# GpSimd multiplies both key pages of a step with the queries in the cached attention, VectorE only sums the products

## The chip, the cores and the metric

The kernel runs on one core of a Trainium2 chip. The core has five engines, each with its own in-order instruction stream: TensorE (matrix products, PE in the profile), VectorE (DVE), ScalarE (ACT), GpSimd (POOL) and SyncE (SP, which here issues most DMAs). They wait for each other through semaphores. The metric is the device time of one execution in microseconds (us), the median of several runs.

## What is computed

One inference step of a decoder layer with two parallel branches, in float32, for a prompt of 1024 tokens and for 8 samples that each continue a cached context of 4096 tokens. The change touches the attention of the 8 samples over their paged cache alone; of the reference that is

```python
def _diff_attend(q, k, v, q_pos, k_pos, lam):
    s = jnp.einsum('nqhmd,nkhmd->nhmqk', q, k).astype(jnp.float32) * (A_DH ** -0.5)
    mask = k_pos[None, :] <= q_pos[:, None]
    p = jax.nn.softmax(jnp.where(mask, s, -jnp.inf), axis=-1)
    p = p[:, :, 0] - lam * p[:, :, 1]
    return jnp.einsum('nhqk,nkhe->nqhe', p.astype(v.dtype), v)
...
        past_k = cache_k[l][page_table].reshape(n_dec, past_len, A_HEADS, A_HD)
        past_v = cache_v[l][page_table].reshape(n_dec, past_len, A_HEADS, A_HD)
```

For each sample there is one query of 4 heads with two sub-queries of 64 each (8 dot products of length 64 with each cached key), 32 pages of 128 keys, and the new key of the step itself. The rest of the layer is a projection of all tokens to 36 blocks of 128 features ("dense"), a causal attention of the prompt with itself, a short convolution with a chunked delta-rule recurrence ("prep" and "solve", 8 tiles of 128 tokens), gates, an output projection, and a recurrent update for the samples.

## The kernel before

Work is staged in three parts that matter here. A first part normalises the tokens and projects queries, keys and values of the prompt (to about 230 us). Then two stages run several streams of work at once. In the first (about 230 to 720 us) they are the dense projection of 20 feature blocks, the attention of the prompt (four heads), and the cached attention of samples 0 to 3. In the second (about 720 to 1310 us) they are the 16 remaining feature blocks, the recurrence with its prep and solve, and the cached attention of samples 4 to 7. The order in which the streams' pieces come is written out once (`phase_a`, `phase_b`, which weave the streams' steps evenly), and every engine goes through this same order with its own share of each piece. Since an engine is in-order, a wait in one stream holds up all others on that engine. A last part (from about 1310 us) projects up, gates and writes the results.

The cached attention (`cached` in each engine's block) takes 16 steps a sample, `gp = j * 16 + i` for step i of sample j, 128 in all. A step covers two key pages, an even and an odd one:

- SyncE loads the two pages into a ring of three pairs (`kring`, semaphores `kin0` to `kin2`). It loads pair gp+3 once both products of gp have been made (`even_mul` and `odd_mul`, L394 and L395). Behind that in its queue come the value pages (ring of six, `load_v`, freed by TensorE's `v_used`), the query broadcasts and the weights of the dense projection.
- GpSimd multiplies the even page (128 keys on partitions, 512 features) with the sample's query, which is broadcast to all partitions (`qB`), into the ring `prod` of four slots, two for each page of two steps (L581). It waits for the even reduction two steps back, which frees its slot.
- VectorE multiplies the odd page in the same way (L1091), then sums the even product in groups of 64 to 8 scores a key (L1093) and the odd one (L1095).
- After 16 steps VectorE adds the score of the step's own key (L1101 to L1103, which write slot 1 of `prod`) and takes the maximum (L1106, `sc_ready`). TensorE and ScalarE do the softmax and the weighted sum of the value pages (L1454) during the next sample's steps.

What stands in the same queues near the change: GpSimd copies the tail of each convolved block (L567, L568), once ScalarE has filled the convolution's buffer (L781); takes powers for the norms (L591, L601, L624); and makes the products of a recurrence tile (L606 to L608, L611 and L612, L615 and L616). VectorE does the convolution's three taps (L1071: multiply a shifted buffer by a weight and add it to the sum, both in SBUF) after ScalarE's L750, the last product of the silu (L1077), the prompt attention's maxima (L1152 to L1154) and combination (L1159 to L1161), and the solve's L1244 to L1268. ScalarE's exponentials are L817, its evacuations L825 to L830. TensorE's dense product is L1425, the prompt attention's L1486, L1499 and L1520, prep's L1542, solve's L1539.

Of the kernel before, what the change touches and what calls it, by code (L numbers as in the profile page):

```python
# [7 lines left out]
ALU = mybir.AluOpType  # L8
# [68 lines left out]
def _program(nc, a, ctx):  # L77
# [65 lines left out]
    s = Semaphores()  # L143
# [31 lines left out]
    kring = sa[:, 0:3072].rearrange("p (u n) -> p u n", u=RK)  # L175
    vring = sa[:, 3072:6168].rearrange("p (u h n) -> p u h n", u=RV, h=AH)
    prod = sa[:, 6168:8216].rearrange("p (u n) -> p u n", u=4)
    qB = sa[:, 8216:9240].rearrange("p (u n) -> p u n", u=2)
# [86 lines left out]
    def v3(ap, n):  # L265
        return ap.rearrange("p (g d) -> p g d", g=n)
# [277 lines left out]
    def _(po):  # L544
# [27 lines left out]
        def cached():  # L572
            for j in range(NS + 1):
                for i in range(SA_STEPS):
                    if j < NS:
                        gp = j * 16 + i
                        po.wait_ge(s["qb_in"], 16 * (j + 1))
                        po.wait_ge(s[f"kin{gp % 3}"], 32 * (gp // 3 + 1))
                        if gp >= 2:
                            po.wait_ge(s["even_red"], gp - 1)  # L580
                        nc.gpsimd.tensor_tensor(prod[:, 2 * (gp % 2), :], kring[:, 2 * (gp % 3), :], qB[:, j % 2, :], ALU.mult).then_inc(s["even_mul"], 1)  # L581
                    yield
            for _ in range(4):
                yield
# [34 lines left out]
        def solve():  # L619
            for t in range(NT):  # L620
                for i in range(SOLVE):
# [3 lines left out]
                    yield  # L625

        gens = dict(dense=dense(), sa=cached(), att=att(), prep=prep(), solve=solve())
        run(ORDER_A, gens)
        run(ORDER_B, gens)
# [327 lines left out]
    def _(dve):  # L957
        nv = [0]

        def link(ins):  # L960
            nv[0] += 1
            ins.then_inc(s["v"], 1)
            dve.wait_ge(s["v"], nv[0])
# [121 lines left out]
        def cached():  # L1085
            def scores(j, i):
                gp, par = j * 16 + i, j % 2
                o = 2 * (gp % 2)
                dve.wait_ge(s["qb_in"], 16 * (j + 1))
                dve.wait_ge(s[f"kin{gp % 3}"], 32 * (gp // 3 + 1))  # L1090
                nc.vector.tensor_tensor(prod[:, o + 1, :], kring[:, 2 * (gp % 3) + 1, :], qB[:, par, :], ALU.mult).then_inc(s["odd_mul"], 1)  # L1091
                dve.wait_ge(s["even_mul"], gp + 1)
                nc.vector.tensor_reduce(sc[:, par, 2 * i, :], v3(prod[:, o, :], 8), AX_X, ALU.add).then_inc(s["even_red"], 1)  # L1093
                dve.wait_ge(s["odd_mul"], gp + 1)
                nc.vector.tensor_reduce(sc[:, par, 2 * i + 1, :], v3(prod[:, o + 1, :], 8), AX_X, ALU.add).then_inc(s["odd_red"], 1)  # L1095

            def maximum(j):
                par = j % 2
                dve.wait_ge(s["odd_red"], 16 * (j + 1))
                dve.wait_ge(s["self_k"], 16 * (j + 1))  # L1100
                nc.vector.tensor_tensor(prod[0:1, 1, :], kself, qB[0:1, par, :], ALU.mult).then_inc(s["self_used"], 1)  # L1101
                dve.wait_ge(s["self_used"], j + 1)
                link(nc.vector.tensor_reduce(sc[0:1, par, NPAGE, :], v3(prod[0:1, 1, :], 8), AX_X, ALU.add))  # L1103
                if j:
                    dve.wait_ge(s["mT_ready"], j)
                nc.vector.tensor_reduce(mx1[:], sc[:, par].rearrange("p g e -> p e g"), AX_X, ALU.max).then_inc(s["sc_ready"], 1)  # L1106

            def softmax(j, i):
                if i == 1:
                    dve.wait_ge(s["mT_ready"], j)  # L1110
                    link(nc.vector.tensor_reduce(mx8[:], ps[0:8, 6, 0:P], AX_X, ALU.max))
                    nc.vector.tensor_scalar(diag8[:], ident[0:8, 0:8], mx8[:], None, ALU.mult).then_inc(s["diag_ready"], 1)
                if i == 3:
                    dve.wait_ge(s["mB_ready"], j)
                    if j >= 2:
                        dve.wait_ge(s["pr_ready"], j - 1)
                    nc.vector.tensor_tensor(scx, sc[:, 1 - j % 2], ps[:, 6, P:P + 8].unsqueeze(1).to_broadcast([P, PAGES, 8]), ALU.subtract).then_inc(s["scx_ready"], 1)

            def combine(m, i):
                if i == 0:  # L1120
                    dve.wait_ge(s["pv_done"], m + 1)
                    if m:
                        dve.wait_ge(s["comb_ready"], m)
                    link(nc.vector.reciprocal(rl[:], ps[:, 7, HD:HD + 1]))
                    nc.vector.tensor_scalar(on[:], ps[:, 7, 0:HD], rl[:], None, ALU.mult).then_inc(s["on_ready"], 1)
                if i == 3:
                    dve.wait_ge(s["comb_ready"], m + 1)
                    nc.vector.tensor_copy(oTs[:, :, m:m + 1], ps[:, 6, 136:136 + AH].unsqueeze(2)).then_inc(s["oTs_ready"], 1)

            for j in range(NS + 1):  # L1130
                for i in range(SA_STEPS):
                    if j >= 2:
                        combine(j - 2, i)
                    if j >= 1:
                        softmax(j, i)
                    if j < NS:
                        scores(j, i)
                        if i == SA_STEPS - 1:
                            maximum(j)
                    yield  # L1140
            for i in range(4):
                combine(NS - 1, i)
                yield
# [644 lines left out]
```

## Time and profile before

| | us |
|---|---|
| runs | 1601.95, 1602.59, 1603.6 |
| median | 1602.59 |
| the profiled execution | 1601.74 |
| its span in the profile | 1600.0 |

The profile is one execution, seen by the hardware profiler. Its span goes from the first instruction to the last; 1.74 us of the execution's own time lie around it. Busy times of engines overlap. A wait is idle time of an engine, put down to what ended it. A duration on VectorE or GpSimd includes the time that the instruction stood still after its start.

### The profile page before, as it was taken

The numbers are of one execution on the slowest core, as the hardware profiler recorded it, in microseconds if no ns is written. First come the engines' busy times: TensorE is split into PE (matmuls) and PEld (weight loads), VectorE is DVE, ScalarE is ACT, GpSimd is POOL, SyncE is SP. The second block draws the span as 40 slices with busy tenths as digits, with TensorE's granted clock in tenths as the row PEclk, the third lists the DMA queues.
The fourth block names the chain that finished last, engine by engine and source line by source line (L and its number), as shares of the span: only waits on it lengthen the run. The fifth ranks groups of instructions, "written<-read, shape, count | busy, mean of one in ns | idle before, by whom it ended". The sixth has DMA issues, their size and how long they took to land.

```text
span 1600.0 us, 23081 instructions
## 1 busy us (share of the span) xinstructions
PE 1422.1 (89%) x8089; PEld 937.1 (59%) x8089; DVE 796.6 (50%) x1411; ACT 297.5 (19%) x850; POOL 357.0 (22%) x257
## 2 busy tenths in 40 slices
PE   3999999988988988986788988989999958959998
PEld 3444866655555555554466766767677745636443
DVE  4546126676776686554565565765533212263001
ACT  2122123223323323222111111121121100000000
POOL 0123101121222131113424324252321100270000
PEclk9999999999999999997999999999999988889999
DMA  7022214444663763665774766767534048214121
GB/s 246 5 83 93 102 52 137 144 128 133 218 204 111 221 215 122 214 212 182 236 241 135 241 201 180 232 186 218 166 113 120 14 156 272 88 44 131 63 79 54
DMA packets 235442, 239.74 MB, mean 150 GB/s; under 512 B 19217, under 2 KB 182902, under 8 KB 234806
## 3 DMA queue, kind: packets, MB, share of 16 engines
q1 hardware_dynamic: 228558, 214.93, 44.0%
q10 hardware_dynamic: 6768, 23.34, 3.7%
q8 instruction: 64, 1.05, 0.3%
q14 instruction: 52, 0.43, 0.1%
HBM read 206.06 MB, written 32.25 MB: 149 GB/s over the span
## 4 chain that ended last, share of the span: by engine, by line
PE 66%; DVE 11%; issue 9%; POOL 5%; DMA 3%; ACT 3%; SPq 2%; DVEq 0%; ACTq 0%; POOLq 0%
PE ps L1425 20%; PE ps L1539 7%; PE ps L1398 7%; PE ps L1708 7%; PE ps L1659 7%; PE ps L1408 4%; PE ps L1486 3%; DVE tr L1071 3%; PE ps L1454 3%; POOL sa L581 2%; DMA sa<-in_cache_v 2%; PE ps L1520 2%; PE ps L1542 1%; DVE sm L1153 1%; PE ps L1364 1%
## 5 line engine op out<-in xcount | busy, mean ns | idle before, releaser
L1425 PE MATMUL ps<-hT,r 128*128 128x344 f32 x1728 | 582.1, 473 | 0.8 <-ACT gb L717 0.8
L1425 PEld LDWEIGHTS ps<-hT,r 128*128 128x128 f32 x1728 | 316.1, 197 | 154.5 <-issue 44.4
L581 POOL TENSOR_TENSOR sa<-sa 128x512 f32<-128x512 f32 x128 | 174.5, 1374 | 336.2 <-DVE sa L1093 305.1
L1398 PE MATMUL ps<-r,hT 128*128 128x512 f32 x256 | 112.2, 593 | 0.0
L1708 PE MATMUL ps<-r,hT 128*128 128x512 f32 x256 | 110.3, 592 | 0.0
L1093 DVE TENSOR_REDUCE sa<-sa 128x8 f32<-128x512 f32 x128 | 86.9, 679 | 43.3 <-POOL sa L581 43.3
L1091 DVE TENSOR_TENSOR sa<-sa 128x512 f32<-128x512 f32 x128 | 102.6, 801 | 2.8 <-DMA sa<-in_cache_k 2.3
L1659 PE MATMUL ps<-tr,r 128*128 128x344 f32 x192 | 66.2, 492 | 42.0 <-DVE hT L1286 22.1
L1454 PE MATMUL ps<-sa 128*2 128x129 f32 x2048 | 77.9, 274 | 24.7 <-DMA sa<-in_cache_v 24.6
L817 ACT ACTIVATE r<-ps,sm 128x128 f32<-128x128 f32 (+7 forms) x64 | 47.1, 739 | 217.7 <-DVE sm L1154 217.7
L1539 PEld LDWEIGHTS ps<-r 128*128 128x128 f32 x576 | 74.0, 193 | 23.1 <-DVE r L1253 5.4
L1095 DVE TENSOR_REDUCE sa<-sa 128x8 f32<-128x512 f32 x128 | 86.4, 675 | 0.0
L1539 PE MATMUL ps<-r 128*128 128x128 f32 x576 | 79.0, 281 | 6.6 <-DVE r L1253 3.9
L1708 PEld LDWEIGHTS ps<-r,hT 128*128 128x128 f32 x256 | 48.6, 190 | 60.9 <-issue 60.7
L1486 PE MATMUL ps<-r 64*128 64x512 f32 (+3 forms) x192 | 67.7, 535 | 16.2 <-ACT r L817 16.2
L1398 PEld LDWEIGHTS ps<-r,hT 128*128 128x128 f32 x256 | 47.6, 190 | 55.6 <-issue 55.6
L1454 PEld LDWEIGHTS ps<-sa 128*2 128x2 f32 x2048 | 41.6, 83 | 64.9 <-DMA sa<-in_cache_v 35.0
L1659 PEld LDWEIGHTS ps<-tr,r 128*128 128x128 f32 x192 | 39.1, 207 | 63.1 <-issue 47.0
L1244 DVE TENSOR_TENSOR tr<-ps,tr 128x512 f32<-128x512 f32 x48 | 33.1, 690 | 85.0 <-PE ps L1539 84.9
L1071 DVE SCALAR_TENSOR_TENSOR tr<-tr,convw 128x1024 f32<-128x1024 f32 x36 | 57.9, 1610 | 22.1 <-ACT tr L750 21.2
L1351 DVE SCALAR_TENSOR_TENSOR tr<-ps,tabs 128x1024 f32<-128x1024 f32 x8 | 9.8, 1225 | 103.6 <-PE ps L1708 103.6
L1659 PE MATMUL ps<-r 128*128 128x344 f32 x192 | 60.2, 457 | 0.0
(265 smaller groups left out, 1768.5 us busy)
## 6 DMA issues: line engine op xcount, KB each, us to landing
sa<-in_cache_k SPq DMA_DIRECT2D x256, 256.0 KB, 3.0
sa<-in_cache_v SPq DMA_DIRECT2D x256, 256.0 KB, 3.5
r<-in_w_f SPq DMA_DIRECT2D x36, 512.0 KB, 4.8
g_dram<-tr ACTq DMA_DIRECT2D x16, 516.0 KB, 4.0
cv_dram<-tr ACTq DMA_DIRECT2D x12, 512.0 KB, 3.0
sa<-g_dram SPq DMA_DIRECT2D x16, 344.0 KB, 3.3
tr<-cv_dram SPq DMA_DIRECT2D x20, 256.0 KB, 4.5
r<-in_x_prompt SPq DMA_DIRECT2D x8, 512.0 KB, 5.0
```

The costliest lines, as they stand in the source:

```text
L581: nc.gpsimd.tensor_tensor(prod[:, 2 * (gp % 2), :], kring[:, 2 * (gp % 3), :], qB[:, j % 2, :], ALU.mult).then_inc(s["even_mul"], 1)
L1071: ins = nc.vector.scalar_tensor_tensor(y, ub[:, k:k + SEQ], convw[:, n, k:k + 1], y, ALU.mult, ALU.add)
L1091: nc.vector.tensor_tensor(prod[:, o + 1, :], kring[:, 2 * (gp % 3) + 1, :], qB[:, par, :], ALU.mult).then_inc(s["odd_mul"], 1)
L1093: nc.vector.tensor_reduce(sc[:, par, 2 * i, :], v3(prod[:, o, :], 8), AX_X, ALU.add).then_inc(s["even_red"], 1)
L1095: nc.vector.tensor_reduce(sc[:, par, 2 * i + 1, :], v3(prod[:, o + 1, :], 8), AX_X, ALU.add).then_inc(s["odd_red"], 1)
L1398: ins = nc.tensor.matmul(ps[:, n % 4, :], hT[:, k, t * P:(t + 1) * P], wt[c][:, k, :], start=(k == 0), stop=(k == KD - 1))
L1425: ins = nc.tensor.matmul(ps[:, 4 + i % 2, 0:G3], wf[f % 4][:, k * P:(k + 1) * P], hT[:, k, cg * G3:(cg + 1) * G3], start=(k == 0), stop=(k ...
L1454: ins = nc.tensor.matmul(ps[32 * h:32 * h + 2, 7, 0:HD + 1], pr[:, p, 2 * h:2 * h + 2], vring[:, v % RV, h, :], start=(p == 0), stop=False ...
L1486: ins = nc.tensor.matmul(ps[:, (m if qb < 4 else 0) + c0 // 512, 0:c1 - c0], QT[r, h, qb * P:(qb + 1) * P], KT[r, h, c0:c1], start=True, s ...
L1539: return heads(lambda o, c: nc.tensor.matmul(o, lhsT[:, c], rhs[:, c], start=True, stop=True), bank)
L1659: ins = nc.tensor.matmul(ps[:, 2 * (n % 2) + m, 0:G3], wup[f][:, (m * AH + k) * P:(m * AH + k + 1) * P], src[:, k, cols], start=(k == 0), ...
L1708: ins = nc.tensor.matmul(ps[:, b0 + hf, :], yT[:, k, t * P:(t + 1) * P], wout[:, k, hf * W:(hf + 1) * W], start=(k == 0), stop=(k == KD - 1))
```

## The change

GpSimd makes the odd product too, right after the even one, and VectorE only sums. GpSimd therefore gets a wait for the odd reduction two steps back, and at the first step of each sample but the first a wait for the sample's maximum before, since the score of the step's own key is worked out in slot 1 of `prod`. VectorE's waits for the query and the key pair go with its multiply. SyncE's code is the same, but `odd_mul` now comes from GpSimd.

```diff
@@ -579,6 +579,11 @@
                         if gp >= 2:
                             po.wait_ge(s["even_red"], gp - 1)
                         nc.gpsimd.tensor_tensor(prod[:, 2 * (gp % 2), :], kring[:, 2 * (gp % 3), :], qB[:, j % 2, :], ALU.mult).then_inc(s["even_mul"], 1)
+                        if gp >= 2:
+                            po.wait_ge(s["odd_red"], gp - 1)
+                        if j and i == 0:
+                            po.wait_ge(s["sc_ready"], j)
+                        nc.gpsimd.tensor_tensor(prod[:, 2 * (gp % 2) + 1, :], kring[:, 2 * (gp % 3) + 1, :], qB[:, j % 2, :], ALU.mult).then_inc(s["odd_mul"], 1)
                     yield
             for _ in range(4):
                 yield
@@ -1086,9 +1091,6 @@
             def scores(j, i):
                 gp, par = j * 16 + i, j % 2
                 o = 2 * (gp % 2)
-                dve.wait_ge(s["qb_in"], 16 * (j + 1))
-                dve.wait_ge(s[f"kin{gp % 3}"], 32 * (gp // 3 + 1))
-                nc.vector.tensor_tensor(prod[:, o + 1, :], kring[:, 2 * (gp % 3) + 1, :], qB[:, par, :], ALU.mult).then_inc(s["odd_mul"], 1)
                 dve.wait_ge(s["even_mul"], gp + 1)
                 nc.vector.tensor_reduce(sc[:, par, 2 * i, :], v3(prod[:, o, :], 8), AX_X, ALU.add).then_inc(s["even_red"], 1)
                 dve.wait_ge(s["odd_mul"], gp + 1)
```

## Rows read from the trace of the kernel before

**Rows 1.** Busy time of each engine in the two stages (start:end, length, engines).
```profile
core 0: us, PE busy (x) PEld busy (x) DVE busy (x) ACT busy (x) POOL busy (x), PEclk, DMA share, GB/s
230.00:720.00 490.00, 449.85 (x2409) 275.72 (x2409) 332.57 (x540) 143.31 (x368) 102.20 (x91) 0.96 0.55 170
720.00:1170.00 450.00, 394.21 (x3039) 294.18 (x3040) 261.61 (x487) 79.81 (x297) 154.54 (x117) 0.94 0.66 199
```
**Rows 2.** The page's costliest groups: busy, mean ns, idle before and its enders.
```profile
L581 POOL TENSOR_TENSOR sa<-sa 128x512 f32<-128x512 f32 x128 | 174.5, 1374 | 336.2 <-DVE sa L1093 305.1
...
L1091 DVE TENSOR_TENSOR sa<-sa 128x512 f32<-128x512 f32 x128 | 102.6, 801 | 2.8 <-DMA sa<-in_cache_k 2.3
```
**Rows 3.** Single lines of code: duration ns minimum/median/maximum.
```profile
L581 POOL TENSOR_TENSOR sa<-sa x128: 1257/1271/2260, 176.0 to 1134.4; 128x512 f32<-128x512 f32 x128
...
L1091 DVE TENSOR_TENSOR sa<-sa x128: 668/686/1774, 228.9 to 1139.3; 128x512 f32<-128x512 f32 x128
...
L1093 DVE TENSOR_REDUCE sa<-sa x128: 666/679/687, 229.5 to 1139.9; 128x8 f32<-128x512 f32 x128
...
L1071 DVE SCALAR_TENSOR_TENSOR tr<-tr,convw x36: 1283/1475/2184, 331.4 to 617.9; 128x1024 f32<-128x1024 f32 x36
```
**Rows 4.** Waits in the first stage (230 to 720): total us, times, longest.
```profile
PE ps L1486 <- ACT r L817: 16.2, 4, 4.5
PE ps L1520 <- ACT junk L830: 15.8, 5, 5.0
...
PE ps L1499 <- DVE r L1161: 1.2, 3, 0.6
```
**Rows 5.** One stall of TensorE in the timeline, from 458 to 467.
```profile
458.09 0.19 POOL L567 COPY utail<-tr 128x3 f32<-128x3 f32 x1 [7.88 <-ACT tr L781]
...
458.37 3.49 POOL L581 TENSOR_TENSOR sa<-sa 128x512 f32<-128x512 f32 x2
...
466.22 0.80 PE L1486 MATMUL ps<-r 64*128 64x256 f32 x2 [4.48 <-ACT r L817]
```
**Rows 6.** The chain of work that ended last, in the same stall (start, us, what).
```profile
459.24 1.49 DVE tr L1071
...
460.76 2.19 DVE tr L1071
...
462.97 1.28 DVE tr L1071
```
**Rows 7.** Waits in the second stage (720 to 1170): total us, times, longest.
```profile
DVE sa L1093 <- POOL sa L581: 43.3, 20, 3.2
...
PE ps L1454 <- DMA sa<-in_cache_v: 22.3, 24, 3.5
...
PE ps L1539 <- DVE r L1247: 9.0, 11, 3.0
...
PE ps L1542 <- DVE tr L1264: 4.4, 1, 4.4
...
PE ps L1539 <- DVE r L1253: 3.9, 2, 2.5
...
PE ps L1539 <- POOL r L616: 1.7, 1, 1.7
```
**Rows 8.** Timeline of another convolution block, 434 to 442: multiplies and taps.
```profile
435.72 4.46 POOL L581 TENSOR_TENSOR sa<-sa 128x512 f32<-128x512 f32 x2
...
435.53 5.73 DVE L1071 SCALAR_TENSOR_TENSOR tr<-tr,convw 128x1024 f32<-128x1024 f32 x3
```
**Rows 9.** Timeline around a late step of the second stage, 851 to 854.
```profile
851.46 0.69 DVE L1093 TENSOR_REDUCE sa<-sa 128x8 f32<-128x512 f32 x1 [2.50 <-POOL sa L581]
...
852.66 0.68 DVE L1264 TENSOR_TENSOR tr<-ps,sm 128x512 f32<-128x512 f32 x1
...
853.39 0.48 PE L1542 MATMUL ps<-ident,tr 128*128 128x128 f32 x1 [4.42 <-DVE tr L1264]
```
**Rows 10.** SyncE's own waits over the whole run: total us, times, longest.
```profile
SPq L395 <- DVE sa L1091: 239.0, 63, 9.2
```
**Rows 11.** Busy time and granted clock right after one stall.
```profile
466.00:472.50 6.50, 6.11 (x13) 3.27 (x14) 6.33 (x14) 2.15 (x8) 1.27 (x1) 0.50 0.48 152
```

## The prediction

> **What bounds the kernel now.** I read the stages first. In the two stages that hold all 128 score steps TensorE is busy 449.85 of 490 us and 394.21 of 450 us [rows 1]: it sets the pace and waits only now and then. VectorE is busy 332.57 and 261.61 us in them, GpSimd 102.20 and 154.54 us, so neither is full. What the change can be worth is therefore read from TensorE's idle time and from who ends it, not from the busy sums.
>
> Next, the costs of one step. GpSimd's multiply stands at 174.5 us for 128, VectorE's at 102.6 us for 128 [rows 2]. Undisturbed, GpSimd's takes 1271 ns and VectorE's 686 ns, but both reach far higher: 2260 and 1774. The reductions never do (666 to 687), and VectorE's convolution taps at L1071, which have two SBUF operands like the multiplies, spread from 1283 to 2184 [rows 3]. So a GpSimd multiply and a VectorE instruction with two SBUF operands delay each other; one with a single SBUF operand is left alone.
>
> Then TensorE's waits. In the first stage nearly all are two kinds: four of 16.2 us behind ScalarE's exponentials and five of 15.8 us behind its L830 [rows 4]. In the trace these are six stalls of 4.5 to 5.0 us (and three short ones), all of one make, of which [rows 5] show one: GpSimd sits in its in-order queue at the copy L567 until ScalarE has filled the convolution buffer; that same event starts VectorE's three taps; GpSimd then runs its two overdue multiplies into the taps. The chain of waits shows what that does: 1.49, 2.19 and 1.28 us [rows 6]. The middle tap has lost 0.9 us. Behind the taps VectorE does the row maxima that the exponentials wait for, and only after those the next score step. In the second stage TensorE waits 22.3 us in 24 pieces for value pages, and 19.0 us behind VectorE's and GpSimd's share of the chunked recurrence (L1247, L1253, L1264, L616). There VectorE also waits 43.3 us in 20 pieces for GpSimd's even multiply [rows 7]: late steps, in which GpSimd's queue had the tile preparation in front.
>
> **What is removed.** 128 multiplies leave VectorE, 102.6 us. Worth is only what of this TensorE waits for. In the six stalls nothing: no L1091 lies between the taps and the maxima, and the taps start when ScalarE's L750 has finished, so earlier savings on VectorE are lost in that wait. Elsewhere in the first stage TensorE waits for VectorE directly for 1.2 us in three pieces (L1161) [rows 4]; I take 0.6. In the second stage eleven waits for L1247 make 9.0 us [rows 7]; two long ones stand behind a late step, where L1091 ran during the wait for GpSimd anyway; the nine others may gain at most 0.69 each, and not more than their own length, so I take 0.2 each, 1.8. Relief: 2.4 us. Its ends are 0 and, if every wait for VectorE or GpSimd in the second stage shrank by 0.69 us (15 pieces) and the 1.2 went, 11.6.
>
> **What is added in the first stage.** GpSimd does two multiplies a step, so four are overdue at each L567, not two. They alternate with the taps, as two back-to-back multiplies already do in another block, where both later taps are hit and the three take 5.73 us [rows 8] instead of the 1.49 + 2.19 + 1.28 = 4.96 of the stall [rows 6]. In the six stalls this hits the last tap too: 2.19 − 1.28 = 0.9 us each, 6 × 0.9 = 5.4 us, straight into TensorE's wait. The six other blocks have no stall, and what their taps lose (0 to 1.8 us) goes into TensorE's work. Lower end 0 (the extra multiplies come after the taps); upper end 3 × 1.27 less the 4.96 − 3 × 1.283 = 1.11 already lost, 2.7 a stall, 16 us.
>
> The Trainium skill ("SBUF — State Buffer", Who interferes with whom) states a rule against this change: a GpSimd instruction and a VectorE one with two SBUF inputs lock the shared port for a whole instruction, and the later one stands still until then. Here the second tap shows 0.9 us lost, less than the multiply's 1.27 us; by the whole instruction the six stalls would give 6 × 1.27 = 7.6 us, an estimate from that page.
>
> **What is added in the second stage.** VectorE now needs even and odd product. Where GpSimd is ahead both are there. In a late step the odd one comes 1.27 us after the even one, of which the even reduction hides 0.6: the step ends 0.65 us later than now. Five of TensorE's stalls stand right behind such a step (one for L1264, two for L1253, two for L1247): 3.3 us. [Rows 9] show one: VectorE waits 2.50 us for GpSimd, reduces twice, does L1264, and TensorE has waited 4.42. In one tile the added multiply stands in front of L615 and L616, for which TensorE waits 1.7 us [rows 7]: 1.3 more. Together 4.6. Ends: 0, and 20 × 1.27 = 25.4 if every late step passes on all of it.
>
> In bursts (three steps in a row behind L606 to L608) the sum is near zero: two multiplies are 2.54 us a step, but VectorE today needs up to 1.77 + 2 × 0.6 = 2.97 there, since it is its own multiply that is blocked (1774 ns [rows 3]; two reductions start to end of turn take 1.2 [rows 9]).
>
> **Waits and queues.** Before each odd multiply GpSimd now waits for the odd reduction two steps back, and once a sample for the maximum (sc_ready). Behind these on GpSimd stand the powers L591 and L601, the tile's products and the copies L567; VectorE, TensorE and ScalarE wait for them. The odd reduction ends 0.6 us after the even one that GpSimd waits for today, the maximum a step ahead of its use, and GpSimd idles over 300 us waiting for VectorE [rows 2], so I cost both at nothing; without that cover it is 7 samples × 1.27 = 8.9 us. SyncE fetches the pages of step gp+3 once both products of gp exist, the value pages behind. Today it waits there 239.0 us for VectorE's multiply [rows 10]; with GpSimd up to two steps ahead it mostly goes on sooner. In late steps it goes on later; I take two such steps at 0.65, 1.3 us, between a loss of 25.4 and a gain of the whole 22.3.
>
> **Sum.** 5.4 + 4.6 + 1.3 − 2.4 = +8.9 us. The profiled execution took 1601.74 us (span 1600.0 and 1.74 around it), so 1610.6; it lies 0.85 below the median of 1602.59, which makes 1611.5. I say 1611.
>
> One cost has no row: TensorE's clock. After such a stall its granted clock is 0.50 for some 6.5 us [rows 11], the lower of its two levels. Whether 0.9 us more idle time lengthens that stretch can't be read off; half as long again, 3.25 us at half speed, costs 1.63 each, 9.8 us for six. I take nothing and keep 9.8 for the range.
>
> **Rivals.**
>
> *GpSimd becomes the bound in the second stage.* Every late step passes on the whole 1.27 us and the clock falls for longer: 5.4 + 25.4 + 9.8 = 40.6 us, 1643; with half of the last two 23 us, 1626. For it: 20 late steps in 64 at half the load. Against: it idles in 295 of those 450 us [rows 1], and 14 of the 20 have no TensorE stall behind them.
>
> *Faster: the key ring lets SyncE go.* If the 239.0 us at L395 are what makes the value pages late, these come sooner and the 22.3 us of waits go: 1602.59 + 5.4 + 4.6 − 2.4 − 22.3 = 1588. It decides from the point where more than half of them go. Against: in front of most of these waits SyncE last waited for TensorE to free a slot, or for nothing.
>
> *No change.* The lost 0.9 us are made good by relief: the stalls fall into a stretch at half clock where TensorE runs slowly anyway, and the late steps gain what L1091 cost. Then 1602.6, give or take 3.2 (0.2%, what a measurement here can tell from none).
>
> **Chances.** Forecast (1606 to 1619) 0.55; GpSimd the bound 0.14; no change 0.17; faster 0.14. So slower 0.69, same 0.17, faster 0.14. The range, 1600 to 1626, leaves about one in ten on each side: it takes in the case of no change with relief near its upper end, and reaches up to GpSimd as the bound at half its price.
>
> **What the profile after would show.** GpSimd near 350 us in 256 multiplies; L1071 at 5.8 to 5.9 us a block instead of 4.96 in the six stalls, and these 5.4 to 5.9 long; VectorE waiting for GpSimd at both reductions, more than 43.3 us together; SyncE's 239.0 us gone from VectorE. The prediction is wrong if the taps don't lengthen, if the stalls stay at 4.5 to 5.0, or if the waits for value pages shrink by over 10 us.

## The result and the profile after

The changed kernel took 1615.65 us in the median of its runs (1612.6 to 1617.12), the kernel before 1602.27 beside it: a ratio of 1.0081 with a 95% interval of 1.0062 to 1.0101, slower by some 13 us. One run of the kernel before, made beside later experiments at a granted clock of 0.736, took 1907.55 us; it is left out of all medians and ratios. The profiled execution took 1614.23 us, its span is 1612.4 us and its mean granted clock 0.946 (before: 1600.0 and 0.953).

First the page's costliest groups that touch the change, after (busy us, mean ns, idle before):

```profile
L581 POOL TENSOR_TENSOR sa<-sa 128x512 f32<-128x512 f32 x128 | 172.1, 1344 | 236.9 <-DVE sa L1095 211.2
L586 POOL TENSOR_TENSOR sa<-sa 128x512 f32<-128x512 f32 x128 | 186.8, 1459 | 2.0 <-DVE mx L1108 2.0
L1095 DVE TENSOR_REDUCE sa<-sa 128x8 f32<-128x512 f32 x128 | 86.9, 679 | 62.4 <-POOL sa L581 62.2
...
L1097 DVE TENSOR_REDUCE sa<-sa 128x8 f32<-128x512 f32 x128 | 86.8, 678 | 16.9 <-POOL sa L586 16.4
...
L1076 DVE SCALAR_TENSOR_TENSOR tr<-tr,convw 128x1024 f32<-128x1024 f32 x36 | 69.7, 1935 | 26.2 <-ACT tr L755 25.3
```

GpSimd now spends 172.1 + 186.8 us in 256 multiplies, against 174.5 in 128 [rows 2]. VectorE has lost its 102.6 us of multiplies and waits 62.2 + 16.4 us for GpSimd's two products. And a line that the diff doesn't touch has changed: the convolution's taps, L1071 before and L1076 now, took 57.9 us on the page of before and take 69.7. Single durations of the taps after (minimum/median/maximum ns):

```profile
L1076 DVE SCALAR_TENSOR_TENSOR tr<-tr,convw x36: 1284/2170/2197, 331.7 to 623.2; 128x1024 f32<-128x1024 f32 x36
```

The median has gone from 1475 [rows 3] to 2170 ns while minimum and maximum stand: the slow tap, rarer than the fast one before, is now the usual one. The two stages after, in the form of [rows 1] (their bounds are moved by the delay so far):

```profile
core 0: us, PE busy (x) PEld busy (x) DVE busy (x) ACT busy (x) POOL busy (x), PEclk, DMA share, GB/s
230.00:726.00 496.00, 448.39 (x2409) 275.04 (x2409) 310.33 (x475) 142.40 (x366) 201.10 (x154) 0.96 0.53 166
726.00:1182.00 456.00, 394.16 (x3041) 295.53 (x3042) 215.56 (x423) 80.01 (x297) 223.78 (x180) 0.94 0.64 196
```

TensorE does the same work. GpSimd is busy 201.10 of 496 us and 223.78 of 456, so it is nowhere the bound. What has grown is TensorE's idle time. Its waits in the first stage, in the form of [rows 4]:

```profile
PE ps L1488 <- ACT r L822: 20.1, 6, 5.5
PE ps L1522 <- ACT junk L835: 18.8, 5, 5.9
PE ps L1501 <- ACT tr L830: 2.6, 2, 1.3
PE ps L1501 <- DVE r L1163: 2.2, 4, 1.2
PE ps L1522 <- ACT tr L830: 1.7, 3, 0.8
```

The first two lines were 16.2 and 15.8 us; their longest pieces have gone from 4.5 and 5.0 us to 5.5 and 5.9. The stall of [rows 5], in the timeline after:

```profile
461.35 0.19 POOL L567 COPY utail<-tr 128x3 f32<-128x3 f32 x1 [5.40 <-ACT tr L786]
...
461.62 1.27 POOL L581 TENSOR_TENSOR sa<-sa 128x512 f32<-128x512 f32 x1
...
462.50 5.88 DVE L1076 SCALAR_TENSOR_TENSOR tr<-tr,convw 128x1024 f32<-128x1024 f32 x3 [1.54 <-ACT tr L755]
...
462.85 2.25 POOL L586 TENSOR_TENSOR sa<-sa 128x512 f32<-128x512 f32 x1
...
465.06 2.24 POOL L581 TENSOR_TENSOR sa<-sa 128x512 f32<-128x512 f32 x1
...
467.26 2.24 POOL L586 TENSOR_TENSOR sa<-sa 128x512 f32<-128x512 f32 x1
...
470.48 0.80 PE L1488 MATMUL ps<-r 64*128 64x256 f32 x2 [5.49 <-ACT r L822]
```

Behind the copy stand four multiplies, and three of them run against the three taps, which take 5.88 us. The chain of waits gives the taps one by one:

```profile
462.50 1.48 DVE tr L1076
...
464.01 2.18 DVE tr L1076
...
466.22 2.17 DVE tr L1076
```

The first two are those of [rows 6] within 0.01; the third has gone from 1.28 to 2.17. In the second stage (720 to 1182), TensorE's waits and VectorE's for GpSimd, in the form of [rows 7]:

```profile
DVE sa L1095 <- POOL sa L581: 62.2, 21, 4.7
...
PE ps L1456 <- DMA sa<-in_cache_v: 20.7, 23, 3.6
...
DVE sa L1097 <- POOL sa L586: 14.7, 30, 0.6
...
PE ps L1541 <- DVE r L1249: 9.0, 11, 2.9
...
PE ps L1541 <- DVE r L1255: 6.9, 3, 2.7
...
PE ps L1544 <- DVE tr L1266: 6.2, 2, 4.7
...
PE ps L1541 <- POOL r L621: 2.5, 1, 2.5
...
PE ps L1541 <- DVE r L1270: 2.2, 1, 2.2
```

The last five lines, TensorE's waits for VectorE and GpSimd, make 26.8 us. Before it was 19.3: the 19.0 of the lines in [rows 7] and 0.3 behind L1250. So +7.5. The late step of [rows 9], after:

```profile
857.12 1.26 POOL L586 TENSOR_TENSOR sa<-sa 128x512 f32<-128x512 f32 x1
857.20 0.69 DVE L1095 TENSOR_REDUCE sa<-sa 128x8 f32<-128x512 f32 x1 [3.01 <-POOL sa L581]
...
858.42 0.69 DVE L1097 TENSOR_REDUCE sa<-sa 128x8 f32<-128x512 f32 x1 [0.54 <-POOL sa L586]
859.02 0.68 DVE L1266 TENSOR_TENSOR tr<-ps,sm 128x512 f32<-128x512 f32 x1
...
859.76 1.11 PE L1544 MATMUL ps<-ident,tr 128*128 128x128 f32 x4 [4.71 <-DVE tr L1266]
```

From the first reduction to the solve's subtraction it takes 859.02 − 857.20 = 1.82 us; in [rows 9] it was 1.20. Between the two reductions VectorE waits 0.54 us for the odd product. Last, SyncE's wait before the key pages, in the form of [rows 10]:

```profile
SPq L395 <- POOL sa L586: 141.8, 42, 12.3
```

For comparing runs I cut the span at three events of the timeline: the first dense product, the first TensorE instruction after the one long wait at the change of stage (for a DMA; 17.9 us before, 18.0 after), and the start of the last dense product. The first stage then takes 509.7 us before and 516.7 after, the second 569.9 and 575.4; the head loses 0.8 and what follows gains 0.7. So +7.0 and +5.5. TensorE's waits, all its idle spells above 0.15 us but that long one, are 38.3 us in the first stage and 44.3 in the second before, and 46.8 and 50.2 after: +8.5 and +5.9. They don't give the stage's length alone, since TensorE also works at a granted clock of 0.50 for part of each stage.

### The profile page after: what moved, and what is told of

It is laid out like the page before. It is cut to its first block, busy times and chain, and to the rows that moved or that the text cites. A ratio compares the mean times of both kernels' runs of the same rounds, so it can differ in the third digit from the quotient of the medians.

```text
span 1612.4 us, 22966 instructions
## 1 busy us (share of the span) xinstructions
PE 1419.8 (88%) x8089; PEld 936.4 (58%) x8089; DVE 728.4 (45%) x1283; ACT 297.3 (18%) x850; POOL 528.5 (33%) x385
## 4 chain that ended last, share of the span: by engine, by line
PE 65%; DVE 11%; issue 8%; POOL 6%; DMA 4%; ACT 3%; SPq 3%; DVEq 0%; ACTq 0%; POOLq 0%
PE ps L1427 20%; PE ps L1400 7%; PE ps L1710 7%; PE ps L1541 7%; PE ps L1661 7%; DVE tr L1076 4%; PE ps L1410 3%; PE ps L1488 3%; PE ps L1456 2%; PE ps L1522 2%; POOL sa L586 2%; DMA sa<-in_cache_v 1%; POOL sa L581 1%; PE ps L1544 1%; DVE sm L1155 1%
## 5 line engine op out<-in xcount | busy, mean ns | idle before, releaser
L581 POOL TENSOR_TENSOR sa<-sa 128x512 f32<-128x512 f32 x128 | 172.1, 1344 | 236.9 <-DVE sa L1095 211.2
L586 POOL TENSOR_TENSOR sa<-sa 128x512 f32<-128x512 f32 x128 | 186.8, 1459 | 2.0 <-DVE mx L1108 2.0
L1095 DVE TENSOR_REDUCE sa<-sa 128x8 f32<-128x512 f32 x128 | 86.9, 679 | 62.4 <-POOL sa L581 62.2
L1661 PE MATMUL ps<-tr,r 128*128 128x344 f32 x192 | 67.0, 497 | 42.0 <-DVE hT L1288 22.1
L1456 PE MATMUL ps<-sa 128*2 128x129 f32 x2048 | 77.6, 276 | 20.9 <-DMA sa<-in_cache_v 20.7
L1097 DVE TENSOR_REDUCE sa<-sa 128x8 f32<-128x512 f32 x128 | 86.8, 678 | 16.9 <-POOL sa L586 16.4
L1076 DVE SCALAR_TENSOR_TENSOR tr<-tr,convw 128x1024 f32<-128x1024 f32 x36 | 69.7, 1935 | 26.2 <-ACT tr L755 25.3
L1456 PEld LDWEIGHTS ps<-sa 128*2 128x2 f32 x2048 | 42.2, 84 | 60.0 <-DMA sa<-in_cache_v 29.3
L559 POOL TENSOR_TENSOR sm<-sm,half 128x8 f32<-128x8 f32 (+1 forms) x17 | 29.1, 1709 | 108.9 <-DVE sm L1028 108.9
L1488 PEld LDWEIGHTS ps<-r 64*128 64x128 f32 x192 | 26.8, 193 | 58.6 <-issue 35.1
```

The lines of the kernel that those rows point to most:

```text
L586: nc.gpsimd.tensor_tensor(prod[:, 2 * (gp % 2) + 1, :], kring[:, 2 * (gp % 3) + 1, :], qB[:, j % 2, :], ALU.mult).then_inc(s["odd_mul"], 1)
L1076: ins = nc.vector.scalar_tensor_tensor(y, ub[:, k:k + SEQ], convw[:, n, k:k + 1], y, ALU.mult, ALU.add)
L1456: ins = nc.tensor.matmul(ps[32 * h:32 * h + 2, 7, 0:HD + 1], pr[:, p, 2 * h:2 * h + 2], vring[:, v % RV, h, :], start=(p == 0), stop=False ...
L1488: ins = nc.tensor.matmul(ps[:, (m if qb < 4 else 0) + c0 // 512, 0:c1 - c0], QT[r, h, qb * P:(qb + 1) * P], KT[r, h, c0:c1], start=True, s ...
L1661: ins = nc.tensor.matmul(ps[:, 2 * (n % 2) + m, 0:G3], wup[f][:, (m * AH + k) * P:(m * AH + k + 1) * P], src[:, k, cols], start=(k == 0), ...
```

## The experiments

All lengths of stages below are of the profiled execution, cut in the same way. One execution gives them to some 3 us: kernels that do the same in the first stage as after take 516.7 to 519.7 us there, and those that do the same in the second 573.4 to 575.8.

| kernel | first stage | second stage | all taps | ratio to before (95% interval) |
|---|---|---|---|---|
| before | 509.7 | 569.9 | 57.9 | |
| after | 516.7 | 575.4 | 69.7 | 1.0081 (1.0062 to 1.0101) |
| first stage only | 517.5 | 569.8 | 69.7 | 1.0044 (1.0028 to 1.0059) |
| second stage only | 510.1 | 575.8 | 57.9 | 1.003 (1.0018 to 1.0042) |
| no odd product | 504.7 | 560.5 | 57.3 | 0.9866 (0.9846 to 0.9886) |
| even product twice | 539.2 | 593.1 | 69.7 | 1.0302 (1.0274 to 1.033) |
| copies on ScalarE, after | 502.6 | 573.4 | 50.2 | 0.9966 (0.9951 to 0.9981) |
| copies on ScalarE, before | 503.9 | 570.4 | 46.8 | 0.9943 (0.9923 to 0.9962) |
| VectorE makes both products | 503.7 | 565.6 | 46.2 | 0.9895 (0.987 to 0.9919) |
| own slot for the self score | 519.7 | 573.4 | 69.7 | 1.0072 (1.0046 to 1.0098) |
| odd product unread | 517.7 | 570.6 | 69.7 | 1.0039 (1.0024 to 1.0054) |
| no odd product, gate kept | 507.9 | 564.1 | 57.2 | 0.9947 (0.9927 to 0.9966) |
| both on VectorE, copies on ScalarE | 503.0 | 567.6 | 46.2 | 0.99 (0.9876 to 0.9924) |

**The two halves apart.** The change for samples 0 to 3 alone (the second kernel has the two conditions the other way round):

```diff
+                        if gp < 64:
+                            if gp >= 2:
+                                po.wait_ge(s["odd_red"], gp - 1)
...
+                            nc.gpsimd.tensor_tensor(prod[:, 2 * (gp % 2) + 1, :], kring[...], qB[...], ALU.mult).then_inc(s["odd_mul"], 1)
...
+                if gp >= 64:
+                    dve.wait_ge(s["qb_in"], 16 * (j + 1))
+                    dve.wait_ge(s[f"kin{gp % 3}"], 32 * (gp // 3 + 1))
+                    nc.vector.tensor_tensor(prod[:, o + 1, :], kring[...], qB[:, par, :], ALU.mult).then_inc(s["odd_mul"], 1)
```

> GpSimd makes the odd product in the first stage alone (samples 0 to 3), VectorE in the second. My theory: the extra multiplies lengthen the taps of the six stalls, 5.7 us as the changed kernel's own trace shows, and little else; 1602.3 + 7 = 1609 us, the six stalls 5.4 to 5.9 us long, the second stage as before. Rival, the loss comes from the second stage alone (late steps) and the first stage's is made good by VectorE's relief: 1602.

> GpSimd makes the odd product in the second stage alone (samples 4 to 7). My theory: late steps end 0.65 us later, 5 stalls behind them, 1.3 for L616 and some for late pages: 1602.3 + 5.5 = 1608 us, the six stalls of the first stage at 4.5 to 5.0 us as before. If both stages' costs simply add, this and the run of the first stage alone together lose the 13 us of the whole change. Rival: GpSimd bound, the second stage carries nearly all of the 13 us: 1615.

They took 1611.82 and 1609.09 us, the kernel before 1603.81 beside them: +0.44% and +0.30%, together +0.74%, within the interval of the whole. Each half lengthens its own stage alone (517.5 and 575.8 us) and leaves the other as it was, so the losses are two and independent.

**VectorE's relief without GpSimd's load.** No engine makes the odd product:

```diff
-                        sp.wait_ge(s["odd_mul"], gp + 1)
...
+        nc.vector.memset(prod, 0.0)
...
-                dve.wait_ge(s["qb_in"], 16 * (j + 1))
-                dve.wait_ge(s[f"kin{gp % 3}"], 32 * (gp // 3 + 1))
-                nc.vector.tensor_tensor(prod[:, o + 1, :], kring[...], qB[:, par, :], ALU.mult).then_inc(s["odd_mul"], 1)
...
-                dve.wait_ge(s["odd_mul"], gp + 1)
```

> The kernel before without any odd product: VectorE's multiply L1091 is left out, the odd reduction sums a zeroed buffer (the scores of the odd keys are left out), SyncE waits for the even product alone. It shows VectorE's relief by itself. My theory: 2.4 us, 1600 us, at most 11.6, 1591. Rival, the key ring lets SyncE go: waits for value pages fall by over 10 us and the time is below 1588.

1584.74 us against 1603.81, 19 us less by the medians and 1.3% or 21 us by the ratio, far more than the 2.4 us of relief in the prediction's sum. But the edit also opens SyncE's gate, so it does two things at once. A later kernel keeps the gate where VectorE's multiply had put it, by making SyncE wait for the even reduction:

```diff
                         sp.wait_ge(s["even_mul"], gp + 1)
-                        sp.wait_ge(s["odd_mul"], gp + 1)
+                        sp.wait_ge(s["even_red"], gp + 1)
                         load_k(gp + 3)
```

> The run without an odd product gained some 20 us, more than the 2.4 that I gave VectorE's relief and more than my upper end of 11.6. This kernel leaves the odd product out in the same way, but SyncE's fetch of the next key pair waits for VectorE's even reduction of the step, as late as VectorE's odd multiply let it go before. If the gain came from the gate of the key ring, it is gone: 1600 and waits for value pages at 22 us again. If it came from VectorE's relief and the multiplies that no longer collide (and the granted clock that follows), it stays: 1585.

1595.39 us against 1603.6, a ratio of 0.9947: the relief alone is worth 8.5 us, and the open gate the rest, some 11 to 13 us. (Relief is here all that goes with VectorE's multiplies, their collisions with GpSimd's too.) The wait at the gate, first in the run that keeps it and then in the one that opens it (both from 230 to 1170):

```profile
SPq L395 <- DVE sa L1090: 244.9, 66, 11.9
```

```profile
SPq L337 <- POOL sa L579: 106.7, 36, 12.2
```

In the same window before, the wait is 233.9 us (239.0 over the whole run [rows 10]), so the first kernel does what it was meant to; in the second the wait is less than half as long. The six stalls are 4.47 to 4.99 us in both, as before. With the gate kept, TensorE's waits in the two stages fall by 4.2 us, from 82.6 to 78.4; the rest of the gain shows as granted clock. Summed over the stretches at 0.50, the first stage has 53.0 us of it before, 47.0 with the gate kept and 57.4 with it open, the second 39.1, 31.5 and 27.9. Whether the relief brings this is not shown: these are single executions, and the mean granted clock of all runs is 0.950 both before and with the gate kept.

**GpSimd's load without the relief.** GpSimd makes the even product twice, VectorE keeps its multiply:

```diff
+                        link(nc.gpsimd.tensor_tensor(prod[:, 2 * (gp % 2), :], kring[...], qB[...], ALU.mult))
                         nc.gpsimd.tensor_tensor(prod[:, 2 * (gp % 2), :], kring[...], qB[...], ALU.mult).then_inc(s["even_mul"], 1)
```

> The kernel before, but GpSimd makes each even product twice into the same slot (nothing left out, VectorE keeps its odd multiply). It adds GpSimd's 1.27 us a step without the relief and without the new waits on reductions and maximum. My theory: the taps meet the same four multiplies, so the six stalls grow by 5.7 us, and each late step by the whole 1.27: 1602.3 + 7 + 8 = 1617. Rival, it is the added waits (odd reduction, maximum) that cost: then about 1604 and stalls as before.

1652.91 us, 3% above before, and well off what was expected. The six stalls are just those of after (5.49 to 5.88 us, all taps 69.7), so it is GpSimd's occupancy that lengthens the taps, with no part in it of the new waits for the odd reduction and the maximum, which this kernel doesn't have. But its stages are 22.5 and 17.7 us longer than those of after, from which it differs by VectorE's multiplies and by one thing more: the even reduction waits here for both of GpSimd's multiplies, in after for the first alone. In its page VectorE's multiplies have grown too, from a mean of 801 ns [rows 2]:

```profile
L1092 DVE TENSOR_TENSOR sa<-sa 128x512 f32<-128x512 f32 x128 | 111.7, 873 | 0.3
```

So with GpSimd doubly loaded the kernel without VectorE's multiply is 40 us shorter (37 by the medians), not 8.5: relief and load don't simply add. TensorE's waits are 18.5 us shorter there (97.0 against 115.5 in the two stages), and its time at 0.50 is 37.5 us less (99.0 against 136.5), by estimate some 19 us at half speed. What of it comes from collisions and what from the later even product these runs don't tell.

**The burst in front of the taps.** GpSimd's two copies, behind which its multiplies pile up, go to ScalarE, which has just filled that buffer; once in the kernel after and once in the one before:

```diff
-                    po.wait_ge(s["f_evac_act"], 3 * (n + 1))
-                    nc.gpsimd.tensor_copy(utail[...], ub[:, SEQ:SEQ + 3].unsqueeze(2))
-                    nc.gpsimd.tensor_copy(sfeat[:, f - 1, :], ub[:, 3 + SEQ:3 + TOK]).then_inc(s["tail"], 1)
...
+            nc.scalar.activation(utail[...], ub[:, SEQ:SEQ + 3].unsqueeze(2), ACT.Copy)
+            nc.scalar.activation(sfeat[:, f, :], ub[:, 3 + SEQ:3 + TOK], ACT.Copy).then_inc(s["tail"], 1)
```

> The changed kernel, with the two small copies L567 and L568 moved from GpSimd to ScalarE, behind its L755 product. GpSimd no longer sits in front of the convolution, so its multiplies are not overdue when the taps start. My theory: the three taps fall from 5.9 us a block towards 3.85, the six stalls from 5.5 to 5.9 us to about 4, so 6 x 1.7 = 10 us off 1615: 1605, less if the copies on ScalarE delay what follows. Rival, the multiplies come when VectorE's reductions free their slots, copies or not: taps and stalls as they are, 1615.

> The kernel before with the same move of the two copies. My theory: taps from 5.0 to 3.85 us in the six stalls, 6 x 1.1 = 6.7 us off: 1596, and the change then costs less than it did. Rival: no effect, 1602, or slower by what the copies cost ScalarE.

1599.69 and 1596.07 us (before: 1604.96). TensorE's two main waits of the first stage, with the change and without it:

```profile
PE ps L1485 <- ACT r L819: 15.0, 4, 5.3
PE ps L1519 <- ACT junk L832: 12.5, 5, 3.9
```

```profile
PE ps L1483 <- ACT r L814: 14.0, 4, 4.4
PE ps L1517 <- ACT junk L827: 12.5, 5, 3.9
```

Both are now shorter than the 16.2 and 15.8 of before [rows 4], and nearly alike; of the six stalls one is longer with the change (5.3 us against 4.4), the others are 3.4 to 3.9 in both. The longer one is the only stall in front of which two multiplies still run into the taps (2300 and 2169 ns). TensorE's waits in the first stage are 31.5 us with the change and 30.2 without, where the copies on GpSimd made it 46.8 and 38.3. So of 8.5 us that the change added to them 1.3 are left: nearly all of its loss there goes through the copies' place in GpSimd's queue. What stays besides that stall is VectorE's wait L1160 (2.4 us, without the change L1158 with 1.0). The lengths of the stage, 502.6 and 503.9, may flatter the change: its execution has only 48.2 us at a clock of 0.50, the other 57.6. By the medians the change now costs 3.6 us, about what its second half alone cost; the second stage takes 573.4 us against 570.4.

**All products on VectorE.** The opposite of the change, so that GpSimd has no share in the scores:

```diff
-                        nc.gpsimd.tensor_tensor(prod[:, 2 * (gp % 2), :], kring[...], qB[...], ALU.mult).then_inc(s["even_mul"], 1)
...
+                nc.vector.tensor_tensor(prod[:, o, :], kring[...], qB[:, par, :], ALU.mult).then_inc(s["even_mul"], 1)
                 nc.vector.tensor_tensor(prod[:, o + 1, :], kring[...], qB[:, par, :], ALU.mult).then_inc(s["odd_mul"], 1)
```

> The other way round: VectorE makes both products, GpSimd none. VectorE gets 88 us more, GpSimd loses 174. If TensorE waits for collisions and late steps and not for VectorE's busy time, as I hold, both go: six stalls at about 3.9 us (6.7 us off), the late steps' 0.65 to 3 us off, but each step on VectorE is 0.69 us longer where it is on the path: 1590 to 1598. Rival, VectorE's load counts: it is busy 33 of 40 us in parts of the first stage, so 128 x 0.69 us more on it cost tens of us: 1620 or more.

1588.59 us, a ratio of 0.9895, just below the 1590 to 1598 that were expected: it beats both kernels, though VectorE has 128 multiplies more. The taps and TensorE's waits in the first stage:

```profile
L1066 DVE SCALAR_TENSOR_TENSOR tr<-tr,convw x36: 1276/1285/1286, 333.9 to 614.7; 128x1024 f32<-128x1024 f32 x36
```

```profile
PE ps L1482 <- ACT r L812: 12.9, 4, 3.4
PE ps L1516 <- ACT junk L825: 12.5, 5, 3.9
PE ps L1495 <- DVE r L1157: 4.6, 4, 1.7
```

All 36 taps take 1276 to 1286 ns: none is slow when GpSimd multiplies nothing. The price of the fuller VectorE stands in the third line (1.2 before), and it is smaller than the gain in the six stalls (3.39 to 3.90 us each). But that is not the whole of the 16 us. Over the two stages TensorE's waits fall only from 82.6 to 78.9 us (those for value pages grow from 22.3 to 26.5 in the second), while its time at 0.50 falls from 92.1 to 71.6, by estimate some 10 us at half speed. This isn't the one execution alone: over all its runs the mean granted clock is 0.956, against 0.951 before. So more of this gain is granted clock than shorter waits, and what raised the clock isn't shown: moving the copies alone in the kernel before shortened the stalls as well and left the mean at 0.949. To this version the move of the copies was added:

> VectorE makes both products and the two copies L567 and L568 are on ScalarE, the two edits that gained alone. My theory: both remove the same burst of GpSimd multiplies into the taps, so the second adds nothing: 1588, stalls at 3.4 to 3.9 us as with either. Rival, their gains of some 17 and 9 us add: 1580.

1587.92 us against 1603.6, a ratio of 0.99, no more than without it, with the same stalls (3.39 to 3.90 us) and the same mean clock of 0.956: the burst can be removed only once.

**The wait for the maximum.** The step's own score is worked out in place instead of in slot 1 of `prod`, so that GpSimd needn't wait for the maximum:

```diff
-                        if j and i == 0:
-                            po.wait_ge(s["sc_ready"], j)
...
-                nc.vector.tensor_tensor(prod[0:1, 1, :], kself, qB[0:1, par, :], ALU.mult).then_inc(s["self_used"], 1)
+                link(nc.vector.tensor_tensor(kself, kself, qB[0:1, par, :], ALU.mult))
+                nc.vector.tensor_reduce(sc[0:1, par, NPAGE, :], v3(kself, 8), AX_X, ALU.add).then_inc(s["self_used"], 1)
...
-                link(nc.vector.tensor_reduce(sc[0:1, par, NPAGE, :], v3(prod[0:1, 1, :], 8), AX_X, ALU.add))
```

> The changed kernel, with the score of the step's own key worked out in place in its own row, so GpSimd needs no wait for the maximum (sc_ready). My theory: the wait had cover, no difference beyond noise, 1615. Rival, the wait holds GpSimd's queue up once a sample: up to 7 x 1.27 = 8.9 us off, 1606.

1615.68 us, a ratio of 1.0072: the time of after. The wait costs nothing that can be measured, as the 2.0 us behind L1108 in the page of after already say.

**The wait for the odd product.** GpSimd makes it as in after, but VectorE sums the query in its place, a tile of the same size, and so never waits for it:

```diff
-                dve.wait_ge(s["odd_mul"], gp + 1)
-                nc.vector.tensor_reduce(sc[:, par, 2 * i + 1, :], v3(prod[:, o + 1, :], 8), AX_X, ALU.add).then_inc(s["odd_red"], 1)
+                nc.vector.tensor_reduce(sc[:, par, 2 * i + 1, :], v3(qB[:, par, :], 8), AX_X, ALU.add).then_inc(s["odd_red"], 1)
...
             def maximum(j):
...
+                dve.wait_ge(s["odd_mul"], 16 * (j + 1))
```

> The changed kernel, but VectorE's odd reduction sums the query buffer and not GpSimd's odd product (the scores of the odd keys are replaced), so no VectorE step waits for the odd product; it is only waited for once a sample, before the maximum. GpSimd's work, its collisions and SyncE's gate stay. My theory: the first stage stays at 516 to 518 us (collisions with the taps) and the second loses part of its 5.5 us, some 3, since late steps no longer end 0.65 us later: 1612. Rival, the second stage's loss too is GpSimd's occupancy (collisions, and the even products behind the odd ones): 1615 and no change in either stage.

1609.49 us against 1603.6, a ratio of 1.0039, that of the kernel with the change in the first stage only (1.0044); their intervals nearly coincide, and that of after (1.0062 to 1.0101) lies above this one. The second stage takes 570.6 us (575.4 after, 569.9 before), the first 517.7, unchanged. TensorE's waits for VectorE and GpSimd in the second stage:

```profile
PE ps L1543 <- DVE r L1251: 8.5, 12, 2.3
PE ps L1543 <- DVE r L1257: 5.6, 3, 2.5
PE ps L1546 <- DVE tr L1268: 4.5, 2, 4.2
PE ps L1543 <- POOL r L622: 2.5, 1, 2.5
PE ps L1543 <- DVE r L1272: 0.5, 1, 0.5
PE ps L1546 <- DVE tr L1216: 0.5, 1, 0.5
```

These make 22.1 us, 4.7 less than after. GpSimd's load is the same in both, so by the medians the second stage's loss comes from waiting for the later odd product, all of it within the noise. Above the 19.3 of before remain 2.8, 0.8 of it in L622, where the added multiply still stands in front of the tile's products. The profiled execution alone wouldn't show this: TensorE's wait for value pages is 24.2 here, 3.5 more than after, so that its waits in the stage fall by 1.5 in all, and the rest of the 4.8 us goes with a time at 0.50 of 34.5 us instead of 42.2.

## Why the prediction was right, point by point

The prediction said slower, 1611 us, between 1600 and 1626; it came to 1615.65. Against its own sum the profiled execution is 1614.23 − 1610.6 = 3.6 us longer: 2.2 of it in the first stage (7.0 where 5.4 − 0.6 was said) and 1.4 in the second (5.5 where 4.6 + 1.3 − 1.8 was said); the rest agrees within 0.1. That the total came so near is in part luck: terms that were too small on both sides, additions and relief, made up for each other.

- **The six stalls, 5.4 us.** Right in mechanism and size. They were 4.47 to 4.99 us and are 5.49 to 5.87, together +5.7. The third tap is hit as [rows 8] showed it for another block. That the burst behind the copies is the cause is shown: without it five of the six stalls are 3.4 to 3.9 us with the change and without, TensorE's waits in the first stage grow by 1.3 us and not by 8.5, and with the load alone and none of the new waits the stalls are the same.
- **The other blocks, taken as work without a stall.** This step failed. Their taps lengthened as well (of the 11.8 us that all taps gained, the six stalls have some 5.3), and short waits behind L830 and L1163 (L825 and L1161 before) went from 1.3 + 0.2 + 1.2 = 2.7 to 2.6 + 1.7 + 2.2 = 6.5 us, +3.8; those behind the exponentials and L835 gained another 1.2. Against that the 2.3 us that TensorE had waited here for value pages went to nothing. The relief of 0.6 at L1161 even had the wrong sign: that wait is L1163 now, 2.2 us. It doesn't come from the burst, as it stays when the copies are moved.
- **The rule of the Trainium skill** ("SBUF — State Buffer", Who interferes with whom), by which the later instruction stands still for a whole one, would, by estimate, have made the stalls 7.6 us longer. Measured are 5.7, and 0.9 a tap: the trace's own figure was the better one.
- **Late steps, 0.65 each.** Right in place and size for one step (1.82 − 1.20 = 0.62). The number of those that TensorE feels was too small: a third wait behind L1255, a second behind L1266 and one behind L1270 came up. With L621 (0.8 more, 1.3 said) TensorE's waits for VectorE and GpSimd grew by 7.5 us, where 4.6 − 1.8 = 2.8 were said. The relief of 1.8 at L1247 didn't come: 9.0 us before, 9.0 after at L1249. That waiting for the odd product makes the loss is shown by the medians of the kernel that doesn't wait for it.
- **Relief, 2.4 us.** Mis-sized, within its ends of 0 to 11.6: alone it is worth 8.5 us. It is nothing in the six stalls, as said. TensorE's waits fell by 4.2 us where 2.4 were said; the rest showed as granted clock, which the prediction had at nothing, and whether the relief caused that is open. Collisions of VectorE's own multiplies (mean 801 ns, 686 undisturbed) entered the sum in the bursts alone, as nothing. So the net was nearer than its terms: if relief and load simply added, the additions would have cost about 22 us, not 11.3; the even product made twice suggests that they don't.
- **SyncE and the value pages, +1.3.** Wrong sign, small: 22.3 us became 20.7, and in the first stage 2.3 became nothing. The rival by which the key ring lets SyncE go has a true core, since an open gate with the odd product left out is worth some 11 to 13 us more than a kept one. The changed kernel gets little of that, as its gate still stands 141.8 us, for GpSimd now.
- **The new waits of GpSimd, nothing.** Right for the maximum: without that wait the time is the same. The wait for the odd reduction wasn't tried alone.
- **The clock, nothing.** About right: the time at 0.50 grew from 53.0 to 56.8 us in the first stage and from 39.1 to 42.2 in the second, 6.9 us in all. By estimate that is some 3.5 us at half speed. The stretch behind the stall that is shown didn't grow: it goes from 465.8 to 472.6 us before and from 468.3 to 475.1 after. Single executions don't tell more: those with the same first stage as after have 54.3 to 62.1 us at 0.50 in it.
- **GpSimd as the bound** didn't happen: it is busy less than half of either stage. **No change** would have needed the relief to outweigh the rest.

## What to carry to other kernels

Before moving work to a less busy engine, look at what that engine does behind its own longest waits: the work piles up there and is let go in one burst, and if the same event starts another engine's two-operand work in SBUF, both slow down exactly where everything waits. Busy sums (45% for VectorE, 33% for GpSimd in the changed kernel) say nothing about that; the timeline around the stalls does. An engine that shares memory with the one you want to relieve can be the thing to empty: here the gain lay in the opposite move, which cost VectorE 128 multiplies and made the kernel about 1% faster, though more of that came as granted clock than as shorter waits. So compare both ways of moving the work, and look at the granted clock of all runs before a gain is put down to a wait.

## What was unexpected of the hardware

In a burst a GpSimd multiply (1.27 us alone) and a tap (1.28 us alone) take turns with great regularity: in the stall shown after, multiplies of 2.24 to 2.25 us start every 2.20 to 2.21 us, and taps of 2.17 to 2.18 in between. A pair thus takes 2.20 us where one after the other would take 2.55; so a part of each runs beside the other, but not the whole. And the same 128 multiplies more on GpSimd cost 13 us where VectorE's went away and some 49 us where they stayed (and each even reduction waited for both), which the single prices on record don't add up to.
